# Side work by weighted steps in the chunk stage of an RWKV-7, retention and attention stack; the turn of YN and the state product at other levels

## The chip, the core and the metric

The kernel runs on one NeuronCore of a Trainium2 chip. The time is device microseconds of one launch, from the first instruction to the last with what lies around them; a profile's span is the first to the last instruction alone. Smaller is better.

## What is computed

The reference is two blocks of two layers each, at batch 1, 512 tokens and width 1024, all in float32. The first block (`hybrid_layer`) runs three branches on one projection of the normed input: a causal pool mixer, retention in chunks of 128 and an RWKV-7 time mix with 8 heads of 64. Three gates mix them, `w_out` projects the result, and an `adaLN` modulation (`w_ada`) surrounds it. The second block is a feed-forward, a conv and attention mixer and another feed-forward, each with a layer norm. The change touches only the RWKV-7 recurrence of the first block:

```python
def step(S, inp):
    r_t, w_t, k_t, v_t, a_t, b_t = inp
    sa = jnp.einsum('bhvk,bhk->bhv', S, a_t)
    S = (S * w_t[:, :, None, :] + sa[..., None] * b_t[:, :, None, :]
         + v_t[..., None] * k_t[:, :, None, :])
    return S, jnp.einsum('bhvk,bhk->bhv', S, r_t)
_, y = lax.scan(step, jnp.zeros((B, H, N, N), jnp.float32), xs)
y = head_norm(y, RWKV_NORM_EPS).reshape(B, T, BRANCH_W) * ln_w + ln_b
```

## The kernel before

**Engines and lanes.** Each engine has a class (`TensorE`, `VectorE`, `ScalarE`, `Pool`, `Sync`) that writes out its own instructions in program order. The classes walk through generators of the same shape (`chunks`, `chunk`, `retention`, `branch`, ...), and each `yield` is a place where `mix` may put in steps of a second generator. So one table of steps sets the order of all four engines, and semaphores, named by keys such as `("cw", at, lv)`, tie them together. An engine works strictly in its own order.

**Weights.** Every large matmul is done in three parts (`three`, L487 to L489): a float32 operand is split into a high and a low half. A unit of weights is 128 by 1024. ScalarE makes its high half (`whi`, L1747) and VectorE its low half (`wlo`, L997, the helper's line that nearly all of VectorE's two-operand work shares). There are four buffers for halves, so a unit is halved when the last matmul of the unit four before it is done. A step of side work is as a rule one `three` of 512 columns; eight of them use up a unit.

**The chunk stage.** It occurs once in each of the two layers of the first block. The main generator is `chunks`: four chunks of 128 tokens by two groups of four heads, eight bodies of `chunk` in a layer. Here the recurrence inside a chunk is a triangular inverse. One body does, on TensorE (its keys in brackets): the products of the chunk, which VectorE masks into `G` and from which it makes the first `U` (cg, L784); turns of B and K (cn); then six levels, n = 2 to 64. A level is a turn of U (ct, L493), which ScalarE copies to X; X by G (cy, L769), which ScalarE copies to Y; and Y by U (cw, L769), which VectorE copies into U (L1399 by a mask, for the last two levels L1405). Then come the product with the state (cW, L816, which needs `SP`, the state times its decay), the solve (cS), the state's update (cK) and the output (cY). VectorE then makes the mean and the variance of the output in `YN`, and GpSimd the inverse root.

**The tail.** The output of a body is finished inside the next one. VectorE scales `YN`, TensorE turns it (cT), ScalarE applies the layer norm's weights (two ACTIVATE into `KH`), and VectorE adds the result into `KH` (`tail_end`), which gives the bank of cT free.

**Banks.** All of these TensorE results go round banks 4 to 7 (`self.ps`). The fourth result after cT takes cT's bank again: with cT behind level 0 that is the turn of U of level 2.

**Side work.** `side` is the rest of the branch work: retention, gates, projections, and the `w_ada` products of two columns. `mix(self.chunks(l), side, 186, SIDE[l])` spreads 345 side steps in layer 0 and 321 in layer 1 evenly over the 186 yields of `chunks` (23 in each body and 2 behind them).

Of the kernel before, what the change touches and what calls it, by code (L numbers as in the profile page):

```python
# [11 lines left out]
ALU = mybir.AluOpType  # L12
# [164 lines left out]
def mix(main, side, main_steps, side_steps):  # L177

    done = n = 0
    for _ in main:  # L180
        n += 1
        while done < side_steps and done * main_steps < n * side_steps:
            next(side, None)
            done += 1
    for _ in range(done, side_steps):
        next(side, None)
# [162 lines left out]
SIDE = (345, 321)  # L349
LEVELS = tuple(enumerate((2, 4, 8, 16, 32, 64)))  # L350
# [103 lines left out]
class TensorE(Lane):  # L454
# [160 lines left out]
    def layer_a(self, l, nxt):  # L615
        k = self.k
        st = ("A", l)
        wa = tuple(x for d in range(8) for x in ((128 * d, 3584, 64), (128 * d, 4672, 64)))
        self.halves([("wa", l), ("wr", l, 0), ("pu", l, 0), ("pz", l, 0)], "w_in", (l,),
                    [wa, t_pieces(3072), t_pieces(0), t_pieces(512)], st)  # L620
        side = itertools.chain(self.pool(l), self.branch(l, 0, 1))
        mix(self.rwkv(l), side, 37, 144)
        drain(side)
        self.at(("ch", l))
        side = itertools.chain(self.retained(l), weave(itertools.chain(
            self.retention(l), self.last_gates(l), self.branch(l, 1, 2), self.out_gates(l)), self.adas_of(l), 8))
        mix(self.chunks(l), side, 186, SIDE[l])
        drain(side)
        self.at(("out", l))
        self.mark(("hlast", nxt))  # L630
        drain(weave(self.branch(l, 2, 8), self.rows(l + 1) if l + 1 < DEPTH else iter(()), 8))
        self.at(("wo", l))
        self.w_out(l, nxt)
# [138 lines left out]
    def chunk(self, l, c, g):  # L772
        k, e = self.k, self.e
        at, last = (l, c, g), (l, c - 1 + g, 1 - g)
        cs = slice(c * 128, (c + 1) * 128)
# [18 lines left out]
        for lv, n in LEVELS:  # L794
            bank = self.bank(self.ps, ("ct", at, lv))
            self.wait_ge(("cu", at, lv))
            self.turn(bank, [U[:, i * 128:(i + 1) * 128] for i in range(4)], ("ct", at, lv))
            yield
            bank = self.bank(self.ps, ("cy", at, lv))
            self.wait_ge(("cx", at, lv))  # L800
            self.four(bank, lambda i: G4[:, i * 512:i * 512 + 128], lambda i: X[:, i * 64:(i + 1) * 64], ("cy", at, lv))
            yield
            bank = self.bank(self.ps, ("cw", at, lv))
            self.wait_ge(("cyy", at, lv))
            self.four(bank, blk(Y), lambda i, n=n: PART(U[:, i * 128:(i + 1) * 128], 1, n), ("cw", at, lv))
            yield
            if lv == 0 and (c or g):
                self.tail(*last)
        S0 = k.SP
        vn = lambda h: k.VN[:, c * 512 + h * 64:c * 512 + (h + 1) * 64]  # L810
# [21 lines left out]
        if c < 3:  # L832
            bank = self.bank(self.ps, ("cK", at))
            self.wait_ge(("cnn", "BN", at), ("cnn", "KN", at), ("cSA", at))
            for i, (h, p, q) in enumerate(heads):
                o = bank[q:q + 64, (p - 2 * g) * 64:(p - 2 * g) * 64 + 64]
                e.matmul(o, k.BN[:, i * 64:(i + 1) * 64], SA(i), start=True, stop=False, skip_group_check=True)
                t = e.matmul(o, k.KN[:, i * 64:(i + 1) * 64], vn(h), start=False, stop=True, skip_group_check=True)
# [155 lines left out]
class VectorE(Lane):  # L994
# [114 lines left out]
    def layer_a(self, l, nxt):  # L1109
        k = self.k  # L1110
        st = ("A", l)
        used = self.halves(st)
        self.wait_ge(*([("xd", t) for t in range(4)] if l else []))
        self.e.memset(k.PP[:, 0:1], 0.0).then_inc(*self.up(("pp0", l)))
        self.give_back(used[:1])
        for i in used[1:]:
            self.spend(i)
        side = itertools.chain(self.pool(l), self.branch(l, 0, 1))
        mix(self.rwkv(l), side, 37, 144)
        drain(side)  # L1120
        self.at(("ch", l))
        side = itertools.chain(self.retained(l), weave(itertools.chain(
            self.retention(l), self.last_gates(l), self.branch(l, 1, 2), self.out_gates(l)), self.adas_of(l), 8))
        mix(self.chunks(l), side, 186, SIDE[l])
        drain(side)
        self.at(("out", l))
        if l + 1 < DEPTH:
            self.mod_columns(l + 1)
        self.rwkv_out(l)
        drain(weave(self.branch(l, 2, 8), self.rows(l + 1) if l + 1 < DEPTH else iter(()), 8))  # L1130
        self.at(("wo", l))
        self.w_out(l, nxt)
# [239 lines left out]
    def chunk(self, l, c, g):  # L1372
# [17 lines left out]
        for lv, n in LEVELS:  # L1390
            yield
            yield
            nb = 64 // n
            wb = k.bank(("cw", at, lv))
            self.wait_ge(("cw", at, lv), ("lmask",))
            if n < 32:
                m = (k.lmask[:, lv * 64:(lv + 1) * 64].rearrange("p (b n) -> p b n", n=n)
                     .unsqueeze(1).broadcast_to([128, 4, nb, n]))
                e.copy_predicated(FOUR_PART(U, 1, n), m, TIGHT(wb, n)).then_inc(  # L1399
                    *self.up(("cu", at, lv + 1), ("free", ("cw", at, lv))))  # L1400
            else:
                for b in range(nb):
                    s = 2 * n * b
                    self.wait_ge()
                    e.tensor_copy(V4(U)[s:s + n, :, s + n:s + 2 * n], TIGHT(wb, n)[s:s + n, :, b, :]).then_inc(  # L1405
                        *self.up(*([("cu", at, lv + 1), ("free", ("cw", at, lv))] if b == nb - 1 else [])))
            yield
            if c or g:
                if lv == 0:
                    self.tail(*last)  # L1410
                if lv == 1:
                    self.tail_end(*last)
        em = k.em[:, 32 * g:32 * g + 32].rearrange("p (t j c) -> p t j c", t=2, j=4)
        bc = lambda j: em[:, :, j, c].unsqueeze(2).broadcast_to([128, 2, 64])
        st = k.st[:, g * 128:(g + 1) * 128].rearrange("p (t v) -> p t v", t=2)
        spt = k.SP[:, :].rearrange("p (t j v) -> p t j v", t=2, j=2)
        if c == g == 0:
            self.wait_ge()
            e.memset(k.SP[:, :], 0.0).then_inc(*self.up())
        for j in range(2) if c else ():  # L1420
            q = slice(64 * j, 64 * j + 64)
            self.wait_ge()
            self.tt(spt[q, :, j, :], st[q, :, :], bc(0)[q, :, :], ALU.mult).then_inc(*self.up(*([("cs", at)] if j else [])))
        yield
        yield
        if c < 3:
# [9 lines left out]
            else:  # L1436
# [16 lines left out]
        self.tt(k.X[:, 256:512].rearrange("p (h n) -> p h n", h=4), vn,  # L1453
                k.bon[:, c * 8 + 4 * g:c * 8 + 4 * g + 4].unsqueeze(2).broadcast_to([128, 4, 64]), ALU.mult).then_inc(*self.up())
        yield

    def tail(self, l, c, g):
        k = self.k
# [280 lines left out]
class ScalarE(Lane):  # L1739
# [68 lines left out]
    def layer_a(self, l, nxt):  # L1808
        k = self.k
        st = ("A", l)  # L1810
        used = self.halves(st)
        self.give_back(used[:1])
        for i in used[1:]:
            self.spend(i)
        self.wait_ge(("x", st, 3), *([("xd", t) for t in range(4)] if l else []))
        side = itertools.chain(self.pool(l), self.branch(l, 0, 1))
        mix(self.rwkv(l), side, 37, 144)
        drain(side)
        self.at(("ch", l))
        side = itertools.chain(self.retained(l), weave(itertools.chain(  # L1820
            self.retention(l), self.last_gates(l), self.branch(l, 1, 2), self.out_gates(l)), self.adas_of(l), 8))
        mix(self.chunks(l), side, 186, SIDE[l])
        drain(side)
        self.at(("out", l))
        self.rwkv_out(l)
        drain(weave(self.branch(l, 2, 8), self.rows(l + 1) if l + 1 < DEPTH else iter(()), 8))
        self.at(("wo", l))
        self.w_out(l, nxt)
# [152 lines left out]
    def chunk(self, l, c, g):  # L1981
        k = self.k
# [9 lines left out]
        for lv, n in LEVELS:  # L1992
            key = ("ct", at, lv)
            self.wait_ge(key, *before)
            self.e.copy(TIGHT(X, n), FOUR_PART(k.bank(key), 0, n)).then_inc(*self.up(("cx", at, lv), ("free", key)))  # L1995
            yield
            key = ("cy", at, lv)
            self.wait_ge(key, ("cz", l))
            self.e.copy(FOUR_PART(Y, 0, n), TIGHT(k.bank(key), n)).then_inc(*self.up(("cyy", at, lv), ("free", key)))  # L1999
            yield  # L2000
            yield
            if lv == 0 and (c or g):
                self.tail(*last)
        key = ("cW", at)
        self.wait_ge(key)
# [200 lines left out]
class Pool(Lane):  # L2206
# [40 lines left out]
    def layer_a(self, l, nxt):  # L2247
# [8 lines left out]
        if l:  # L2256
# [7 lines left out]
        self.e.memset(k.Y[:, :], 0.0).then_inc(*self.up(("cz", l)))  # L2264
        side = itertools.chain(self.retained(l), weave(itertools.chain(
            self.retention(l), self.last_gates(l), self.branch(l, 1, 2), self.out_gates(l)), self.adas_of(l), 8))
        mix(self.chunks(l), side, 186, SIDE[l])
        drain(side)
        self.at(("out", l))
        self.wait_ge(*ALL(("out", l)))  # L2270
# [47 lines left out]

    def chunk(self, l, c, g):
        hs = self.k.hs  # L2320
        yield from self.steps(22)
        self.rstd(hs[:, 8:12], hs[:, 4:8], 1.0 / 64, 64e-5, [("cvar", (l, c, g))], ("crs", (l, c, g)))
        yield

# [151 lines left out]
```

## Time and profile before

| | before |
|---|---|
| median of 3 runs | 3810.29 us (3807.25 to 3812.89) |
| the profiled execution's own time | 3813.6 us |
| its span | 3811.8 us |
| mean granted TensorE clock | 0.951 |
| chunk stage of layer 0 | about 341 to 870 us |
| chunk stage of layer 1 | about 1206 to 1706 us |

The two stages can be found in the trace by the tile U, which is used nowhere else. A wait in the trace is idle time of an engine right before an instruction, with the engine, tile and line whose end let it go.

### The profile page before, as it was taken

The page shows a single profiled execution, that of the slowest core. Times are in us where ns is not written, and L with a number is a line of the kernel's source. Part 1 is how long each engine was busy: PE and PEld are TensorE (multiplying, and loading weights), DVE is VectorE, ACT ScalarE, POOL GpSimd, SP SyncE. Part 2 cuts the span into 40 slices and gives each one's busy share as a digit, 9 for nine tenths or more (in the row PEclk, how much of TensorE's full clock was granted, in tenths as well). Part 3 has the DMA queues.
Part 4 walks back from the last instruction along what each step waited for, and adds up shares of the span by engine and source line. Part 5 has one row for each costly group of instructions (what it writes and reads, how often), then busy time and mean ns, then how long its engine had stood idle before and what let it go on. Part 6 is the DMA issues. An engine that isn't in the chain of part 4 may idle for free. (4 is left out here: it accounts for less than half of the span.)

```text
span 3811.8 us, 43469 instructions
## 1 busy us (share of the span) xinstructions
PE 3462.5 (91%) x17192; PEld 2808.8 (74%) x17192; DVE 1790.3 (47%) x2485; ACT 1147.3 (30%) x1671; POOL 174.5 (5%) x232
## 2 busy tenths in 40 slices
PE   4889888988888888989999977999999997889999
PEld 2767777776667767778888855888888886668887
DVE  5564554346655554345333474533243327644333
ACT  3433223222343222223332224223122312333321
POOL 1000000000000000000000110000000002000000
PEclk7989999999999999999999987999999999889999
DMA  4122111223222111122323211232323321113232
GB/s 167 61 74 76 56 56 63 76 72 103 89 72 72 56 56 39 46 79 81 102 97 107 96 45 34 83 100 95 107 86 100 101 98 64 50 45 100 99 106 78
DMA packets 83803, 303.72 MB, mean 80 GB/s; under 512 B 9856, under 2 KB 10128, under 8 KB 83600
## 3 DMA queue, kind: packets, MB, share of 16 engines
q1 hardware_dynamic: 78048, 282.59, 22.3%
q0 software_dynamic: 5552, 18.35, 1.5%
q8 instruction: 136, 2.23, 0.2%
q14 instruction: 67, 0.55, 0.0%
HBM read 296.19 MB, written 4.72 MB: 79 GB/s over the span
## 5 line engine op out<-in xcount | busy, mean ns | idle before, releaser
L487 PE MATMUL bank<-hh,whi 128*128 128x512 f32 (+1 forms) x2880 | 1133.3, 393 | 99.2 <-DVE wlo L997 40.1
L489 PE MATMUL bank<-hh,wlo 128*128 128x512 f32 (+1 forms) x2880 | 1090.3, 379 | 0.0
L488 PE MATMUL bank<-hl,whi 128*128 128x512 f32 (+1 forms) x2880 | 1090.0, 378 | 0.0
L997 DVE TENSOR_TENSOR wlo<-raw,whi 128x1024 fp32r<-128x1024 f32 x530 | 650.3, 1227 | 932.9 <-ACT whi L1747 864.9
L1747 ACT CAST whi<-raw 128x1024 fp32r<-128x1024 f32 x530 | 556.2, 1049 | 839.6 <-PE bank L489 722.3
L487 PEld LDWEIGHTS bank<-hh,whi 128*128 128x128 f32 x2880 | 559.4, 194 | 223.8 <-issue 72.5
L489 PEld LDWEIGHTS bank<-hh,wlo 128*128 128x128 f32 x2880 | 558.5, 194 | 98.8
L488 PEld LDWEIGHTS bank<-hl,whi 128*128 128x128 f32 x2880 | 560.0, 194 | 85.2 <-issue 3.6
L487 PE MATMUL bank<-whi,fh 128*128 128x512 f32 x704 | 278.3, 395 | 0.0
L489 PE MATMUL bank<-whi,fl 128*128 128x512 f32 x704 | 277.8, 395 | 0.0
L488 PE MATMUL bank<-wlo,fh 128*128 128x512 f32 x704 | 277.7, 395 | 0.0
L997 DVE TENSOR_TENSOR tmp<-tmp,bank 128x512 f32<-128x512 f32 x104 | 71.6, 688 | 244.0 <-PE bank L489 241.6
L2076 ACT CAST fh<-tmp 128x512 fp32r<-128x512 f32 x88 | 54.6, 621 | 375.4 <-DVE tmp L997 375.4
L487 PEld LDWEIGHTS bank<-whi,fh 128*128 128x128 f32 x704 | 132.6, 188 | 30.9
L489 PEld LDWEIGHTS bank<-whi,fl 128*128 128x128 f32 x704 | 132.6, 188 | 30.8
L488 PEld LDWEIGHTS bank<-wlo,fh 128*128 128x128 f32 x704 | 132.7, 188 | 30.7
L769 PEld LDWEIGHTS bank<-X,G 128*128 128x128 f32 x768 | 107.1, 206 | 22.6 <-ACT X L1995 14.4
L493 PE MATMUL bank<-ident,U 128*128 128x128 f32 x384 | 62.9, 289 | 56.2 <-DVE U L997 26.3
L769 PEld LDWEIGHTS bank<-U,Y 128*128 128x128 f32 x768 | 98.7, 192 | 20.0 <-ACT Y L1999 13.2
L1399 DVE COPY_PREDICATED U<-lmask,bank 128x256 f32<-128x256 uint32 x64 | 32.5, 508 | 170.7 <-PE bank L769 169.8
L769 PE MATMUL bank<-X,G 128*128 128x64 f32 x768 | 106.6, 286 | 5.6 <-ACT X L1995 5.4
L493 PEld LDWEIGHTS bank<-ident,U 128*128 128x128 f32 x384 | 46.2, 146 | 79.3 <-DVE U L997 33.2
(302 smaller groups left out, 3850.5 us busy)
## 6 DMA issues: line engine op xcount, KB each, us to landing
raw<-in_W SPq DMA_DIRECT2D x530, 512.0 KB, 3.3
bc<-in_ln_g POOLq DMA_DIRECT2D x6, 512.0 KB, 4.3
bc<-in_ln_b POOLq DMA_DIRECT2D x6, 512.0 KB, 5.5
xn<-in_x SPq DMA_DIRECT2D x4, 512.0 KB, 8.6
xn<-in_x POOLq DMA_DIRECT2D x4, 512.0 KB, 5.5
xd<-xn POOLq DMA_DIRECT2D x4, 512.0 KB, 3.4
xn<-xd POOLq DMA_DIRECT2D x4, 512.0 KB, 5.3
out<-xn SPq DMA_DIRECT2D x4, 512.0 KB, 2.6
```

Source lines behind the costliest of these rows:

```text
L487: e.matmul(out, ah, bh, start=first, stop=False, skip_group_check=True)
L488: e.matmul(out, ah, bl, start=False, stop=False, skip_group_check=True)
L489: return e.matmul(out, al, bh, start=False, stop=last, skip_group_check=True)
L493: t = self.e.transpose(bank[:, j * 128:(j + 1) * 128], x, self.k.ident[:, :])
L769: t = self.e.matmul(bank[:, i * 64:(i + 1) * 64], lhs(i), rhs(i), start=True, stop=True, skip_group_check=True)
L997: return self.e.tensor_tensor(o, a, b, op)
L1399: e.copy_predicated(FOUR_PART(U, 1, n), m, TIGHT(wb, n)).then_inc(*self.up(("cu", at, lv + 1), ("free", ("cw", at, lv))))
L1747: self.e.copy(self.k.halves(i)[0], self.k.raw_unit(n)).then_inc(*self.up(("hi", i)))
L2076: self.e.copy(HALF(k.fh, m), tm).then_inc(*self.up(("fh", st, m)))
```

## The change

`mix` now adds up what the main generator yields: a plain `yield` counts 1, a `yield 2` counts 2. The yield behind cw in each of the six levels becomes `yield 2`, on all four engines. The total goes from 186 to 234 (29 in each body and 2), and the number of side steps stays the same, so a plain yield gets 345/234 = 1.47 steps instead of 1.85 in layer 0, and the yield behind cw gets 2.95. The tail of the body before (the scaling and turn of `YN`) moves from behind level 0 to behind level 1. Its end (`tail_end`) moves from behind level 1 to behind level 2. The product of the state with its decay (`SP`), which stood behind level 5, becomes a method `state` and stands behind level 3.

```diff
 def mix(main, side, main_steps, side_steps):
     done = n = 0
-    for _ in main:
-        n += 1
+    for w in main:
+        n += w or 1
         while done < side_steps and done * main_steps < n * side_steps:
             next(side, None)
             done += 1
...
-        mix(self.chunks(l), side, 186, SIDE[l])
+        mix(self.chunks(l), side, 234, SIDE[l])
...
             self.four(bank, blk(Y), lambda i, n=n: PART(U[:, i * 128:(i + 1) * 128], 1, n), ("cw", at, lv))
-            yield
-            if lv == 0 and (c or g):
+            yield 2
+            if lv == 1 and (c or g):
                 self.tail(*last)
...
-            yield
+            yield 2
             if c or g:
-                if lv == 0:
+                if lv == 1:
                     self.tail(*last)
-                if lv == 1:
+                if lv == 2:
                     self.tail_end(*last)
+            if c and lv == 3:
+                self.state(l, c, g)
...
-        for j in range(2) if c else ():
-            q = slice(64 * j, 64 * j + 64)
-            self.wait_ge()
-            self.tt(spt[q, :, j, :], st[q, :, :], bc(0)[q, :, :], ALU.mult).then_inc(*self.up(*([("cs", at)] if j else [])))
...
+    def state(self, l, c, g):
+
+        k = self.k
+        st = k.st[:, g * 128:(g + 1) * 128].rearrange("p (t v) -> p t v", t=2)
+        spt = k.SP[:, :].rearrange("p (t j v) -> p t j v", t=2, j=2)
+        before = k.em[:, 32 * g:32 * g + 32].rearrange("p (t j c) -> p t j c", t=2, j=4)[:, :, 0, c].unsqueeze(2).broadcast_to(
+            [128, 2, 64])
+        for j in range(2):
+            q = slice(64 * j, 64 * j + 64)
+            self.wait_ge()
+            self.tt(spt[q, :, j, :], st[q, :, :], before[q, :, :], ALU.mult).then_inc(*self.up(*([("cs", (l, c, g))] if j else [])))
...
             self.e.copy(FOUR_PART(Y, 0, n), TIGHT(k.bank(key), n)).then_inc(*self.up(("cyy", at, lv), ("free", key)))
             yield
-            yield
-            if lv == 0 and (c or g):
+            yield 2
+            if lv == 1 and (c or g):
                 self.tail(*last)
...
-        yield from self.steps(22)
+        yield from self.steps(2)
+        for _ in LEVELS:
+            yield from self.steps(2)
+            yield 2
+        yield from self.steps(2)
```

What this does to the order is shown at three places. The first is VectorE in the third body of layer 0 (c = 1, g = 0), from the copy of level 1 on. `qr`, `sw` and the BN instructions are retention's, `wlo` is a low half. Before:

```order
L1399 COPY_PREDICATED U<-lmask,bank 128x64x4
L997 TENSOR_TENSOR KH<-KH,bank 128x2x128
L1399 COPY_PREDICATED U<-lmask,bank 128x32x8
L997 TENSOR_TENSOR qr<-bank,cosr 128x512
L997 TENSOR_TENSOR sw<-bank,sinr 64x512 x2
L997 TENSOR_TENSOR qr<-qr,sw 128x512
L1264 BN_STATS stat<-bank 128x6 x4
L1267 BN_AGGR stat<-stat 128x2 x4
L997 TENSOR_TENSOR wlo<-raw,whi 128x1024 x2
L1399 COPY_PREDICATED U<-lmask,bank 128x16x16
```

After, the same stretch of VectorE:

```order
L1399 COPY_PREDICATED U<-lmask,bank 128x64x4
L997 TENSOR_TENSOR YN<-YN,hs 128x256
L1399 COPY_PREDICATED U<-lmask,bank 128x32x8
L997 TENSOR_TENSOR qr<-bank,cosr 128x512
L997 TENSOR_TENSOR sw<-bank,sinr 64x512 x2
L997 TENSOR_TENSOR qr<-qr,sw 128x512
L1264 BN_STATS stat<-bank 128x6 x4
L1267 BN_AGGR stat<-stat 128x2 x4
L997 TENSOR_TENSOR wlo<-raw,whi 128x1024 x2
L997 TENSOR_TENSOR KH<-KH,bank 128x2x128
L1399 COPY_PREDICATED U<-lmask,bank 128x16x16
L1000 TENSOR_SCALAR sw<-bank,stat 128x128 x4
```

The addition into `KH`, which frees the bank of cT, stood right behind the copy of level 1 and now stands behind retention's block and two low halves. The second place is TensorE at the same point, from cw of level 2 (the first row) to the turn of U of level 3 (L493). L726 is retention's product. Before:

```order
L769 MATMUL bank<-U,Y 128x64 x4
L487 MATMUL bank<-hh,whi 128x512
L488 MATMUL bank<-hl,whi 128x512
L489 MATMUL bank<-hh,wlo 128x512
L487 MATMUL bank<-hh,whi 128x512
L488 MATMUL bank<-hl,whi 128x512
L489 MATMUL bank<-hh,wlo 128x512
L493 MATMUL bank<-ident,U 128x128 x4
L726 MATMUL bank<-vret,pt 128x128 x10
```

After:

```order
L769 MATMUL bank<-U,Y 128x64 x4
L487 MATMUL bank<-hh,whi 128x512
L488 MATMUL bank<-hl,whi 128x512
L489 MATMUL bank<-hh,wlo 128x512
L487 MATMUL bank<-hh,whi 128x512
L488 MATMUL bank<-hl,whi 128x512
L489 MATMUL bank<-hh,wlo 128x512
L726 MATMUL bank<-vret,pt 128x128 x10
L487 MATMUL bank<-hh,whi 128x512
L488 MATMUL bank<-hl,whi 128x512
L489 MATMUL bank<-hh,wlo 128x512
L493 MATMUL bank<-ident,U 128x128 x4
```

Two steps before the turn of U have become three steps and retention's product. The third place is TensorE at the start of the last body of layer 1, from the last product of the chunk (L784) to the turns of B and K. Before:

```order
L784 MATMUL bank<-AR,KH 128x256
L487 MATMUL bank<-hh,whi 128x512
L488 MATMUL bank<-hl,whi 128x512
L489 MATMUL bank<-hh,wlo 128x512
L487 MATMUL bank<-hh,whi 128x512
L488 MATMUL bank<-hl,whi 128x512
L489 MATMUL bank<-hh,wlo 128x512
L493 MATMUL bank<-ident,BH 128x128 x2
L493 MATMUL bank<-ident,KH 128x128 x2
```

After:

```order
L784 MATMUL bank<-AR,KH 128x256
L487 MATMUL bank<-hh,whi 128x512
L488 MATMUL bank<-hl,whi 128x512
L489 MATMUL bank<-hh,wlo 128x512
L493 MATMUL bank<-ident,BH 128x128 x2
L493 MATMUL bank<-ident,KH 128x128 x2
```

One step less lies between them. Counted over the whole order of TensorE in both stages, in steps of three matmuls (a mean over the 16 bodies, or the 96 levels):

| from, to | before | after |
|---|---|---|
| turn of U, X by G (ct to cy) | 1.58 | 1.25 |
| X by G, Y by U (cy to cw) | 1.50 | 1.22 |
| cw to the next turn of U, no tail between | 1.59 | 2.45 |
| cw to the turn of YN | 1.36 | 2.64 |
| end of a body to cg | 1.50 | 0.93 |
| cg to the turns of B and K | 1.62 | 1.44 |
| those to the first turn of U | 1.69 | 1.19 |

## Rows read from the trace of the kernel before

**Rows 1.** Page: busy us, share and instructions of each engine

```profile
PE 3462.5 (91%) x17192; PEld 2808.8 (74%) x17192; DVE 1790.3 (47%) x2485; ACT 1147.3 (30%) x1671; POOL 174.5 (5%) x232
```

**Rows 2.** Windows of the two chunk stages (times, span, engines' busy us, clock)

```profile
341.00:870.00 529.00, 473.95 (x2772) 384.10 (x2772) 235.18 (x394) 147.69 (x259) 25.94 (x29) 0.95 0.20 66
1206.00:1706.00 500.00, 446.43 (x2676) 365.17 (x2676) 217.66 (x380) 129.45 (x237) 22.36 (x29) 0.97 0.16 54
```

**Rows 3.** Waits of TensorE, 341 to 1706: total us, times, longest

```profile
PE bank L493 <- DVE U L997: 26.3, 14, 5.6
PE bank L493 <- DVE YN L997: 20.8, 9, 5.3
PE bank L493 <- DVE KH L997: 11.7, 9, 2.6
PE bank L493 <- DVE U L1405: 10.7, 7, 3.5
...
PE bank L816 <- DVE SP L997: 7.7, 5, 3.3
PE bank L493 <- DVE U L1399: 7.4, 7, 3.1
...
PE bank L769 <- ACT X L1995: 5.4, 8, 1.2
...
PE bank L493 <- DVE G L997: 5.1, 9, 2.5
PE bank L769 <- ACT Y L1999: 4.8, 8, 1.4
```

**Rows 4.** Timeline: turns of YN behind the last body of each layer

```profile
843.53 0.44 PE L493 MATMUL bank<-ident,YN 128*128 128x128 f32 x2 [2.86 <-DVE YN L997]
...
1678.03 0.56 PE L493 MATMUL bank<-ident,YN 128*128 128x128 f32 x2 [2.84 <-DVE YN L997]
```

**Rows 5.** Timeline: one halving ahead of the copy of U (layer 1)

```profile
1583.87 0.37 ACT L1999 COPY Y<-bank 128x256 f32<-128x256 f32 x1 [1.31 <-PE bank L769]
...
1584.33 1.05 ACT L1747 CAST whi<-raw 128x1024 fp32r<-128x1024 f32 x1
...
1585.51 1.22 DVE L997 TENSOR_TENSOR wlo<-raw,whi 128x1024 fp32r<-128x1024 f32 x1 [1.05 <-ACT whi L1747]
...
1586.77 0.43 DVE L1399 COPY_PREDICATED U<-lmask,bank 128x256 f32<-128x256 uint32 x1
...
1587.23 0.42 DVE L997 TENSOR_TENSOR KH<-KH,bank 128x256 f32<-128x256 f32 x1
...
1587.70 0.55 PE L493 MATMUL bank<-ident,U 128*128 128x128 f32 x3 [0.90 <-DVE KH L997]
```

**Rows 6.** Timeline: retention's block on VectorE behind level 2, third body of layer 0

```profile
494.59 0.60 PE L493 MATMUL bank<-ident,U 128*128 128x128 f32 x4
494.86 0.69 DVE L997 TENSOR_TENSOR qr<-bank,cosr 128x512 f32<-128x512 f32 x1 [1.01 <-PE bank L489]
495.02 2.40 PE L726 MATMUL bank<-vret,pt 128*128 128x128 f32 x20
...
497.17 0.48 PE L487 MATMUL bank<-hh,whi 128*128 128x512 f32 x1
...
500.01 2.54 DVE L997 TENSOR_TENSOR wlo<-raw,whi 128x1024 fp32r<-128x1024 f32 x2
...
502.58 0.45 DVE L1399 COPY_PREDICATED U<-lmask,bank 128x256 f32<-128x256 uint32 x1
```

**Rows 7.** Timeline of TensorE behind a wait of 4.50 us

```profile
535.85 1.09 PE L493 MATMUL bank<-ident,U 128*128 128x128 f32 x4 [4.50 <-DVE U L997]
536.58 0.78 PE L487 MATMUL bank<-hh,whi 128*128 128x512 f32 x1
...
541.73 0.40 PE L489 MATMUL bank<-hh,wlo 128*128 128x512 f32 x1
541.96 0.39 PE L487 MATMUL bank<-hh,whi 128*128 128x512 f32 x1
```

More of the change, by code:

```diff
@@ L1123, in layer_a @@
             self.retention(l), self.last_gates(l), self.branch(l, 1, 2), self.out_gates(l)), self.adas_of(l), 8))
-        mix(self.chunks(l), side, 186, SIDE[l])
+        mix(self.chunks(l), side, 234, SIDE[l])
         drain(side)
@@ L1415, in chunk @@
         st = k.st[:, g * 128:(g + 1) * 128].rearrange("p (t v) -> p t v", t=2)
-        spt = k.SP[:, :].rearrange("p (t j v) -> p t j v", t=2, j=2)
         if c == g == 0:
@@ L1821, in layer_a @@
             self.retention(l), self.last_gates(l), self.branch(l, 1, 2), self.out_gates(l)), self.adas_of(l), 8))
-        mix(self.chunks(l), side, 186, SIDE[l])
+        mix(self.chunks(l), side, 234, SIDE[l])
         drain(side)
@@ L2266, in layer_a @@
             self.retention(l), self.last_gates(l), self.branch(l, 1, 2), self.out_gates(l)), self.adas_of(l), 8))
-        mix(self.chunks(l), side, 186, SIDE[l])
+        mix(self.chunks(l), side, 234, SIDE[l])
         drain(side)
```

## The prediction

> **What bounds the kernel now.** I read the page first: TensorE is busy for 91% of the span, VectorE for 47%, ScalarE for 30% [rows 1]. No work is added or taken away by this change, so the time can only move through TensorE's idle time and its clock. Second, the windows of the two chunk stages, the only places where the order changes: of 529 and 500 us TensorE is busy 473.95 and 446.43, so 108.6 us are idle, and VectorE is busy for 44% of both, with a granted clock of 0.95 and 0.97 [rows 2]. No engine is the bound there but TensorE. Third, the waits of TensorE over that stretch, sorted by who ended them. The reader is to see that nearly all end with VectorE's handing over something of the chunk: the first U of a body 26.3 us, the masked G 5.1, YN 20.8, the copies of U inside the levels 7.4 and 10.7, the addition into KH 11.7, SP 7.7; ScalarE's X and Y cost 5.4 and 4.8 [rows 3]. All of these name instructions that only the chunk stages have. The DMA does not appear.
>
> VectorE is not short of time; it is late because in its own order something long stands ahead of the piece that TensorE wants. So what counts is what stands ahead of each such piece, and how much TensorE has to do meanwhile (its cover). A `three` step is worth 3 x 0.23 = 0.70 us (two matmuls start at 541.73 and 541.96) [rows 7].
>
> **The change part by part.**
>
> *SP.* The state product goes two levels forward. Its five waits, 7.7 us [rows 3], end: behind level 3 it has two levels of TensorE work ahead of its first reader. It costs VectorE nothing new. **-7.7 us.**
>
> *Turn of YN, one level later.* Of the 20.8 us [rows 3], 2.86 and 2.84 are those behind the last bodies [rows 4], which don't move. That leaves 15.1. At level 1 the order shows five bodies with side work between the copy of U and YN (two with two low halves, one with a low half and a `pt`, two with retention's four `sw`), and the 1.28 steps of cover that are added behind cw help all bodies. I put what remains at 10, from the chain priced below (the double halvings 2.5 and 3.9, the one with `pt` 1.7, lateness elsewhere 2): **-5 us**, between -15 and 0.
>
> *Turns of U.* From cw to the next turn the cover grows from 1.59 to 2.45 steps, 0.6 us. The waits on the two copies are 7.4 + 10.7 = 18.1 us in 14 pieces [rows 3]. 14 x 0.6 would be 8.4. Besides, side work now falls behind the copy more often, where a whole level covers it. Against that, a block ahead of the copy has less cover in the other two gaps. **-9 us**, between -4 and -15.
>
> *Bank of cT.* This is where I see the loss. The turn of U that comes three results later waits until `tail_end` has added into KH. Before, `tail_end` stood behind level 1, and in the order of VectorE nothing stood between the copy of U and it in all but two of the 14 bodies that have it inside. After, it stands behind level 2, with three steps' worth of side work ahead of it, and the order shows side work there in 11 of 14 (about 31 us of VectorE's time by the rows' durations, where it was under 2). This work can't be hidden behind a level: `tail_end` must come before the next turn of U, and the cover is the gap alone.
> The price of one halving there: ScalarE's high half 1.05, VectorE's low half 1.22, KH 0.42, with the hand-overs some 2.9 us [rows 5], from the end of the unit; cover is the rest of the gap, 0.7 to 2.1 us. So 0.8 to 2.2 us each, 0.6 more where ScalarE has a gate's sigmoid first. Those rows show the same with the halving ahead of cw: a wait of 0.90 at twice the cover. Nine bodies are of about this kind or have a small block; worked through one by one, about 17 us.
> Three bodies have retention's block. The first of these is the place shown in the order: the block starts when its unit ends at 494.59, and its low halves end at 500.01 + 2.54 = 502.55, 8.0 us later. KH makes it 8.4. Before, it stood ahead of the copy of level 3 and had a whole level as cover, and the copy at 502.58 held nobody up [rows 6]. After, TensorE has ahead of the turn of U retention's product, 497.17 - 495.02 = 2.15 us [rows 6], and one step: 2.85. A wait of about 5.5 us. The same block in layer 1 with one low half less makes 4.3; the second half of the block (the third body's successor, `kr`, `ol`, `wlo` ahead of KH) about 4.8. Together 14.6.
> 32 in place of 11.7: **+20 us**. Below, +5 (if VectorE runs the block in the gaps of its waits for TensorE), above +24.
>
> *Start of a body.* From the output to the first turn of U TensorE has 1.50 + 1.62 + 1.69 = 4.81 steps before and 0.93 + 1.44 + 1.19 = 3.56 after, 1.25 less, 0.87 us. VectorE's part (YN, G, U) is fixed and already the longer one: G and the first U hold TensorE for 31.4 us, U in 14 of 16 bodies [rows 3]. 14 x 0.87 = 12.2; some 3 us of side work leave VectorE's stretch with it. **+9 us**, between +4 and +12.
>
> *X, Y and the end of a body.* Gaps of one step rather than two become the rule on the two copies of ScalarE. They cost 10.2 us over 192 gaps [rows 3], few of them long. A high half that falls between two copies (1.05 us [rows 5]) was covered by 1.4 us and is not by 0.7. **+4 us**, between 0 and +10.
>
> *Clock.* Behind the wait of 4.50 us the granted clock is at the lower level, 1.2 GHz: four transposes take 1.09 us [rows 7] instead of 0.60 [rows 6], and the upper level, 2.4 GHz, is back about 5 us later (0.39 per matmul). Such a stretch gives away half its length, some 2 us. Waits above 2.4 us are about as many as before by my list (SP's and YN's go, KH's come): **0**, between -6 and +6.
> The Trainium skill, page "TensorE: Matmul & The Clock Gate", section "HAM oscillation — how this bites in real kernels", says the same of the price: the extra wall time is the throttled time times (1 - 1.2/2.4). The trace agrees at that place. By this rule the change would pay wherever it breaks up the longest waits, even at equal idle time; that is a rival below.
>
> Sum: -7.7 - 5 - 9 + 20 + 9 + 4 = +11.3. Neighbouring waits overlap (while TensorE stands at KH, ScalarE and VectorE catch up for the next X, Y and U), for which I take off 3: **+8 us**. The profiled execution took 3813.6, which is 3.3 above the median; against it that is 3821.6, against the median of 3810.3 it is 3818.
>
> The Trainium skill, page "Perfetto Trace Analysis", section "Optimization Strategy", advises to find the gaps of the busiest engine, see which semaphore ends them, and let that dependency start sooner. By it the turn of U is the right target (18.1 us). The rows say it is a fifth of the idle time, and that more hangs on the start of a body and on KH.
>
> **The rivals.** (A measurement of this kernel tells 0.2%, 7.6 us, from no change.)
>
> *1. Forecast: the waits for KH and at the start of a body outweigh the gains.* +3 to +20 us. Chance 0.53, two thirds of it above the 7.6.
>
> *2. The other side, faster: the gap behind cw really is the place where lateness is made.* For it: SP and YN are gains that I can name by instruction, together up to 7.7 + 15.1 = 22.8, and the turns of U give up to 15. Against it: the block at 494.86. It decides at KH. If its waits stay at about 12 us, the sum is +11.3 - 20 = -9, so 3802; with the U and YN terms at their best ends -25, 3785. The point at which the sign turns is KH at 20 us. Chance 0.22.
>
> *3. A draw: the idle time only changes its name.* VectorE's long blocks are the same and meet TensorE's next hand-over wherever that is; the nine small cases come out at 1 us rather than 1.9. Then KH stands at about 24, the sum is near +1, 3811. Chance 0.17.
>
> *4. The clock.* The clock falls short by 0.05 x 529 + 0.03 x 500 = 41 us in the two stages, a part of it while TensorE stands still [rows 2], and the long waits at SP and YN (up to 3.3 and 5.3 [rows 3]) are of the kind that rows 7 show. If four or five stretches of 2 us go and none comes, 8 to 10 us are gained beside rival 3's balance: 3802. If the KH waits of 4 to 5.5 us and longer ones at the first U (5.6 now [rows 3]) each draw one, 6 more are lost on top of the forecast: 3824. The gain has a chance of 0.03, the loss one of 0.05.
>
> **The numbers.** Most likely 3818. The forecast's own range is 3813 to 3830. The range for 8 in 10 reaches into rivals 2 and 4: 3799 to 3832. Faster by over 0.2% (below 3802.7): rival 2 and the gain of 4, 0.25. Slower (above 3817.9): two thirds of the forecast and the loss of 4, 0.40. Within: the rest, 0.35.
>
> **What would show it.** In the waits of TensorE: SP gone; YN about 16 with the two tails; L1399 and L1405 together about 9; KH from 11.7 to 25 or more, with single waits of 4 to 5 us in the third and fourth body of layer 0 and the fourth of layer 1, right behind retention's product; first U and G at about 40; X and Y at 13 to 16. The clock of the two windows stays at 0.95 to 0.97. I am wrong if KH stays below 20 or the start of a body doesn't move; in the first case `tail_end` runs earlier than its place in the order makes me think.

## The result, and the profile after

The changed kernel takes 3844.65 us, median of 4 runs (3841.62 to 3848.38), beside 3810.78 us for the kernel before in the same comparison. The ratio is 1.0091, with a 95% interval of 1.0076 to 1.0107: slower by 34 us. The direction was forecast; the size was not, and lies outside the range. The profiled execution took 3841.62, its span 3839.8.

The page of the changed kernel, busy time by engine, answers to [rows 1]. TensorE is busy 16 us longer with the same instructions:

```profile
PE 3478.6 (91%) x17192; PEld 2817.9 (73%) x17192; DVE 1790.2 (47%) x2485; ACT 1148.0 (30%) x1671; POOL 175.5 (5%) x232
```

The windows of the two chunk stages of the changed kernel (times, length, then busy us of TensorE, its weight loads, VectorE, ScalarE and GpSimd, the granted clock, DMA share, GB/s) answer to [rows 2]:

```profile
338.50:879.00 540.50, 481.16 (x2772) 386.72 (x2773) 237.27 (x397) 149.03 (x261) 29.09 (x33) 0.94 0.21 65
1214.00:1739.00 525.00, 461.70 (x2676) 375.22 (x2676) 217.43 (x379) 129.26 (x237) 23.87 (x32) 0.94 0.16 51
sum 1065.50, PE 942.86 PEld 761.95 DVE 454.71 ACT 278.29 POOL 52.96; mean PE 471.43 PEld 380.97 DVE 227.35 ACT 139.15 POOL 26.48
```

Cut at the same events (341 to 872 and 1208 to 1708), the stages of the kernel before are 1031.0 us with TensorE busy for 920.4. So the stages hold the whole loss, 34.5 us (the two profiled executions are 28.0 us apart; outside the stages the changed one is 6.5 us shorter), and it has two parts: idle time goes from 110.6 to 122.6 (+12.0), and busy time from 920.4 to 942.9 (+22.5) for equal work. The clock of the two windows fell from 0.95 and 0.97 to 0.94 and 0.94.

The waits of TensorE from 341 to 1730 (in total, times, longest, us) answer to [rows 3]:

```profile
PE bank L493 <- DVE KH L997: 33.5, 12, 5.4
PE bank L493 <- DVE U L997: 28.1, 14, 7.0
PE bank L493 <- DVE YN L997: 22.1, 13, 4.4
...
PE bank L769 <- ACT X L2004: 7.8, 13, 1.6
...
PE bank L493 <- DVE U L1405: 5.2, 4, 2.0
PE bank L769 <- ACT Y L2008: 5.1, 7, 2.0
...
PE bank L493 <- DVE G L997: 4.6, 10, 2.1
...
PE bank L493 <- DVE U L1399: 2.2, 2, 1.2
```

SP is gone from the list, and KH has become its head. The timeline at the place where the prediction put the largest wait for KH, both engines, is the next view (start, duration, engine, line, operation, tiles, count, and in brackets the idle time before). VectorE works off two low halves, then adds into KH, and only then may the turn of U take the bank:

```profile
485.96 2.54 DVE L997 TENSOR_TENSOR wlo<-raw,whi 128x1024 fp32r<-128x1024 f32 x2
...
488.54 0.42 DVE L997 TENSOR_TENSOR KH<-KH,bank 128x256 f32<-128x256 f32 x1
489.01 1.12 PE L493 MATMUL bank<-ident,U 128*128 128x128 f32 x4 [5.38 <-DVE KH L997]
...
491.21 1.80 PE L769 MATMUL bank<-X,G 128*128 128x64 f32 x8
...
494.19 0.63 PE L487 MATMUL bank<-hh,whi 128*128 128x512 f32 x1
...
494.62 0.44 PE L488 MATMUL bank<-hl,whi 128*128 128x512 f32 x1
494.90 0.39 PE L489 MATMUL bank<-hh,wlo 128*128 128x512 f32 x1
```

Behind the wait four transposes take 1.12 us and a 512-column matmul 0.63, where they take 0.60 and 0.39 at the upper level; that lasts 5.6 us. Such a stretch can also follow a shorter wait and last longer, as TensorE's timeline of the changed kernel shows at 634:

```profile
634.33 0.84 PE L493 MATMUL bank<-ident,U 128*128 128x128 f32 x4 [2.37 <-DVE KH L997]
...
636.38 1.86 PE L595 MATMUL bank<-ones,gate 2*128 2x1 f32 x8
638.17 1.97 PE L769 MATMUL bank<-X,G 128*128 128x64 f32 x8
...
641.33 1.80 PE L769 MATMUL bank<-U,Y 128*128 128x64 f32 x8
...
644.31 0.63 PE L487 MATMUL bank<-hh,whi 128*128 128x512 f32 x1
...
645.05 0.40 PE L489 MATMUL bank<-hh,wlo 128*128 128x512 f32 x1
```

This one is 10.4 us long. The granted clock of the trace has the same place at 0.50, and at 1.00 behind it (the same columns as in the windows above):

```profile
634.66:644.88 10.22, 10.22 (x38) 8.78 (x37) 1.01 (x3) 0.91 (x3) 0.00 (x0) 0.50 0.16 53
644.90:654.90 10.00, 10.00 (x60) 7.80 (x59) 1.79 (x3) 2.76 (x5) 0.00 (x0) 1.00 0.16 52
```

In the text from here on, **low clock** is the time in the two stages over which the 512-column matmuls of the `three` steps take more than 0.6 us, each stretch counted from the first such matmul to the next faster one: 55.7 us before, 89.2 after. Half of the difference, 16.7 us, is its price. This measure misses the edges of the stretches. **Granted low** is TensorE's busy time inside the stretches over which the trace's granted clock is 0.50: 72.6 us before, 115.8 after. Half of that difference is 21.6 us, so the clock is nearly all of the 22.5.

Which stretches grew can be listed by the durations, if every product is counted and not the 512-column ones alone (which gives 66.0 us before and 99.8 after). Two stretches followed a wait for KH before, 6.9 us; seven do after, 43.5 us. All others together went from 59.1 to 56.3. So the low clock that was added lies behind the waits for KH. That the waits are its cause is shown by e4_end_first, below.

### The profile page after: what moved, and what is told of

The parts are those of the page before. It is cut to its first block and busy times, and to the rows that moved or that the text cites. A ratio compares the mean times of both kernels' runs of the same rounds, so it can differ in the third digit from the quotient of the medians.

```text
span 3839.8 us, 43480 instructions
## 1 busy us (share of the span) xinstructions
PE 3478.6 (91%) x17192; PEld 2817.9 (73%) x17192; DVE 1790.2 (47%) x2485; ACT 1148.0 (30%) x1671; POOL 175.5 (5%) x232
## 3 DMA queue, kind: packets, MB, share of 16 engines
q1 hardware_dynamic: 78048, 282.59, 22.5%
## 5 line engine op out<-in xcount | busy, mean ns | idle before, releaser
L1399 DVE COPY_PREDICATED U<-lmask,bank 128x256 f32<-128x256 uint32 x64 | 32.6, 509 | 230.4 <-PE bank L769 229.8
L493 PE MATMUL bank<-ident,U 128*128 128x128 f32 x384 | 64.5, 294 | 69.0 <-DVE KH L997 33.5
L493 PEld LDWEIGHTS bank<-ident,U 128*128 128x128 f32 x384 | 48.2, 150 | 90.3 <-DVE KH L997 38.7
```

What stands on the lines that cost most here:

```text
L493: t = self.e.transpose(bank[:, j * 128:(j + 1) * 128], x, self.k.ident[:, :])
```

## The experiments

The kernel before ran beside each group of them, with medians of 3810.8 to 3814.7, so small differences are read from the ratios. Idle time is the stages' length less TensorE's busy time, from the two windows of each run; the expectations' idle time is the sum of the waits with a known releaser, some 4 us less. Times are us.

| kernel | median | ratio to before, 95% | stages | busy | idle | low clock | granted low |
|---|---|---|---|---|---|---|---|
| before | 3810.8 | | 1031.0 | 920.4 | 110.6 | 55.7 | 72.6 |
| changed | 3844.7 | 1.0091 (1.0076 to 1.0107) | 1065.5 | 942.9 | 122.6 | 89.2 | 115.8 |
| e1_state | 3801.5 | 0.9967 (0.9957 to 0.9977) | 1020.6 | 918.3 | 102.3 | 49.9 | 72.2 |
| e2_tail | 3836.2 | 1.0058 (1.0039 to 1.0077) | 1051.2 | 926.1 | 125.1 | 61.7 | 85.5 |
| e3_weights | 3847.0 | 1.0087 (1.0066 to 1.0107) | 1068.8 | 943.5 | 125.3 | 102.0 | 118.7 |
| e4_end_first | 3798.7 | 0.9958 (0.9945 to 0.9971) | 1020.3 | 926.6 | 93.7 | 63.1 | 84.0 |
| e5_tail_back | 3807.8 | 0.9983 (0.9974 to 0.9993) | 1023.5 | 921.3 | 102.3 | 58.6 | 73.7 |
| e6_both_first | 3793.5 | 0.9943 (0.9928 to 0.9958) | 1016.2 | 930.5 | 85.7 | 75.7 | 92.7 |
| e7_even_both_first | 3781.5 | 0.9916 (0.9901 to 0.9931) | 1003.7 | 909.2 | 94.5 | 40.3 | 54.5 |
| e8_w3 | 3788.5 | 0.9938 (0.9923 to 0.9953) | 1010.2 | 924.2 | 86.0 | 58.0 | 73.5 |
| e9_w15 | 3780.0 | 0.9915 (0.9901 to 0.9930) | 996.9 | 909.3 | 87.7 | 44.1 | 53.8 |
| e10_even_tail0 | 3785.2 | 0.9929 (0.9914 to 0.9943) | 1005.5 | 909.3 | 96.2 | 44.8 | 52.7 |
| e11_w2_ct | 3818.7 | 1.0019 (1.0009 to 1.0028) | 1040.1 | 932.0 | 108.1 | 87.4 | 98.6 |
| e12_filled | 3774.4 | 0.9901 (0.9885 to 0.9918) | 996.7 | 923.1 | 73.7 | 38.1 | 54.5 |

### One part at a time

**e1_state**: the kernel before, with the product of the state and its decay behind level 3.

```diff
+            if c and lv == 3:
+                self.state(l, c, g)
...
```

> The kernel before with one part of the change: the state product (SP) behind level 3 of the inversion in place of behind level 5. Theory A (the loss of the change lies in the addition into KH, which now stands behind a gap full of side work, and in the low-clock stretches that its waits draw): this part is a plain gain. The five SP waits (7.7 us) go, and with the two of 2.9 and 3.3 us perhaps two low-clock stretches of 4 us, worth 2 us each: 3799 to 3804. Theory B (the loss comes from the uneven spread of the side steps itself: shorter plain gaps at the start of a body and around X and Y): the same here. Rival to both: the wait only moves on to the next hand-over of VectorE, 3808 to 3812.

The waits for SP are gone and no other moved by more than 0.5 us. The stages are 10.4 us shorter.

**e2_tail**: the kernel before, with the tail and its end one level later, in even steps.

```diff
             yield
-            if lv == 0 and (c or g):
+            if lv == 1 and (c or g):
                 self.tail(*last)
...
             yield
-            if c or g:
-                if lv == 0:
-                    self.tail(*last)
-                if lv == 1:
-                    self.tail_end(*last)
+            if (c or g) and lv == 1:
+                self.tail(*last)
+            if (c or g) and lv == 2:
+                self.tail_end(*last)
...
```

> The kernel before with one part of the change: the tail one level later (YN turned behind level 1, its end behind level 2), with even steps. In the order about 18 us of VectorE's side work stand ahead of the addition into KH in 7 of the 14 bodies that have it inside (under 2 us in 2 bodies before, about 31 us in 11 bodies in the changed kernel). Theory A: the KH waits rise from 11.7 to 20 to 26 us, two of them at 5 us, YN falls by 8 to 12 us; 3806 to 3820. Theory B: moving the tail is harmless and YN's gain shows: 3800 to 3804.

Slower by 22 us, more than either theory had; this part alone makes the kernel slower. KH goes from 11.7 to 25.1, as theory A had it, but YN only from 20.8 to 17.7, and L1399 goes up from 7.4 to 11.2.

**e3_weights**: the kernel before, with `yield 2` behind cw and the total of 234, and nothing else of the change.

> The kernel before with one part of the change: weight 2 behind each level's last product, with tail and state product where they were. Theory A: KH waits stay at 10 to 17 us, YN at 15 to 22, the copies of U fall from 18 to about 9, the start of a body costs a few us more; 3806 to 3822. Theory B: this part carries most of the loss: 3832 to 3846.

Theory A fell as it was worded. The turns of U do gain (L1399 and L1405 together 7.1, from 18.1), but what the change puts first in the list of waits is SP:

```profile
PE bank L493 <- DVE U L997: 30.1, 15, 7.0
PE bank L816 <- DVE SP L997: 25.1, 8, 7.1
PE bank L493 <- DVE YN L997: 18.6, 7, 4.6
```

The double portion of side work behind level 5 stands ahead of the state product, which its readers want at once. In the full change the state had moved away from there.

**e5_tail_back**: the changed kernel with the tail where it was: weights and the early state.

```diff
             yield 2
-            if lv == 1 and (c or g):
+            if lv == 0 and (c or g):
                 self.tail(*last)
...
             yield 2
-            if c or g:
-                if lv == 1:
-                    self.tail(*last)
-                if lv == 2:
-                    self.tail_end(*last)
+            if (c or g) and lv == 0:
+                self.tail(*last)
+            if (c or g) and lv == 1:
+                self.tail_end(*last)
...
```

> The changed kernel with the tail where it was (YN turned behind level 0, its end behind level 1); weights and the early state product stay. Set against the changed kernel it prices the move of the tail under weights, set against the run with weights alone it prices the state product under weights. In that run KH cost 16.1 us, YN 18.6 and SP 25.1. If the waits add up without moving: SP's 25 go, KH and YN stay near 16 and 19, idle time of the two stages about 97 us against 118 in the changed kernel, time 3808 to 3822. If the waits only move on to the next hand-over, or if the spread of steps is itself the loss: 3830 and above.

This closes the decomposition. From before to e1_state the early state gives -0.33% (-12.6 us). From there to e5_tail_back the weights cost 0.16% (+6), and the two intervals overlap. From there to the changed kernel the tail's later level costs 1.08% (+41). The last step is 42.0 us in the stages: 20.3 of idle time (KH 16.1 to 33.5, YN 18.6 to 22.1) and 21.6 of busy time, with the low clock going from 58.6 to 89.2 and granted low from 73.7 to 115.8. And e3_weights less e5_tail_back, which differ in the state's place alone, is 45.3 us in the stages, again half idle (23.0) and half busy time (22.2).

### The order inside the gap

**e4_end_first**: the changed kernel with `tail_end` right behind the copy of level 2, ahead of the gap's side work.

```diff
+            if (c or g) and lv == 2:
+                self.tail_end(*last)
             yield 2
-            if c or g:
-                if lv == 1:
-                    self.tail(*last)
-                if lv == 2:
-                    self.tail_end(*last)
+            if (c or g) and lv == 1:
+                self.tail(*last)
```

> The changed kernel with one edit: VectorE makes the addition into KH (tail_end) right behind the copy of level 2, ahead of the weighted gap's side work, not behind it. All engines' other work stays in its order. Theory A: the KH waits (33.5 us in the changed kernel) fall to under 5 us, and the low-clock time in the two stages goes back towards that of before (mean granted clock of the two stages from 0.94 back to 0.95 to 0.97); 3800 to 3815. Theory B: the KH waits go but come back under other names, and the time stays at 3832 or above.

3798.66 us: 46 us less than the changed kernel by the medians, 51 by the ratios (0.9958 beside 1.0091) and 45.2 in the stages, by the place of one instruction per body. At the block of the prediction the timeline of e4_end_first reads:

```profile
479.67 0.43 DVE L1399 COPY_PREDICATED U<-lmask,bank 128x256 f32<-128x256 uint32 x1 [5.94 <-PE bank L769]
...
480.13 0.42 DVE L997 TENSOR_TENSOR KH<-KH,bank 128x256 f32<-128x256 f32 x1
...
480.84 2.39 PE L726 MATMUL bank<-vret,pt 128*128 128x128 f32 x20
481.11 0.69 DVE L997 TENSOR_TENSOR qr<-bank,cosr 128x512 f32<-128x512 f32 x1 [0.55 <-PE bank L489]
...
483.76 0.60 PE L493 MATMUL bank<-ident,U 128*128 128x128 f32 x4
```

The addition stands ahead of retention's block, and the turn of U starts without a wait at the upper level. KH falls from 33.5 to 1.4 us. The stages lose 28.9 us of idle time and 16.3 of busy time, and granted low falls from 115.8 to 84.0, of which half is 15.9: a microsecond of waiting for KH cost 1.4.

**e6_both_first**: as e4_end_first, and the scaling of YN too stands ahead of the gap's side work, behind the copy of level 1.

> The changed kernel with both of VectorE's parts of the tail ahead of the weighted gap's side work: the scaling of YN right behind the copy of level 1, the addition into KH right behind that of level 2. Against the run with only the latter, YN's waits inside the bodies (16 us) fall to about 3: 12 to 16 us less and perhaps some low-clock time, 3780 to 3790. If the wait only moves on to the next hand-over of VectorE: 3795 to 3800.

YN falls from 22.1 to 12.0, not to 3, and idle time to 85.7. But busy time rises by 3.9, and of the 10 us won in waits 5 arrive by the medians and 4.1 in the stages; the two ratios' intervals overlap. The time lies between the two ranges expected.

**e7_even_both_first**: the same with even steps (plain yields, total 186): the changed kernel's two moves without its weights, and both of VectorE's parts ahead of the side work.

> As the run before this one, but with even steps (weight 1): state product behind level 3, tail one level later, both of VectorE's parts of the tail ahead of the gap's side work. It prices the weights with the tail and the state product out of their way. If the weights are a gain once nothing stands behind the gap (the copies of U in time), this is 4 to 12 us slower than the weighted one. If they cost (starts of bodies, X and Y, and small products packed closer, with more time at the lower clock for the same idle time), it is 3 to 12 us faster than the weighted one, 3772 to 3785, with the low-clock stretches of the two stages at 50 us or less in all, where the weighted kernels so far have 63 to 102.

12 us faster than e6_both_first although it has 8.8 us more idle time. The copies of U are waited for 22.2 us again (11.5 and 10.7; 18.1 before the change); against that stand 21.3 us less busy time. The windows of e6_both_first, then those of e7_even_both_first:

```profile
338.10:854.80 516.70, 474.32 (x2773) 381.38 (x2773) 237.33 (x397) 149.27 (x261) 29.18 (x33) 0.95 0.21 68
1189.80:1689.30 499.50, 456.14 (x2676) 372.04 (x2677) 217.41 (x379) 129.46 (x237) 24.11 (x33) 0.95 0.17 53
```

```profile
339.90:856.20 516.30, 465.82 (x2772) 378.37 (x2773) 237.29 (x397) 149.26 (x261) 28.07 (x33) 0.96 0.21 68
1192.00:1679.40 487.40, 443.35 (x2677) 364.86 (x2677) 217.42 (x379) 129.48 (x237) 24.14 (x33) 0.98 0.17 55
```

**e10_even_tail0**: as e7_even_both_first with the tail at levels 0 and 1.

> Even steps, both parts first, the state behind level 3, and the tail where it stood before the change (levels 0 and 1). Theory A, the tail's level is worth little once both parts stand ahead of the gap's side work: KH 4 to 12 us, YN 15 to 19 us, within 8 us of the kernel with even steps and the tail one level later, 3780 to 3792 us. Theory B, the later level itself pays: 3795 us or more.

3785.2, ratio 0.9929 beside 0.9916 with the later level: the intervals overlap. KH is 9.0 and YN 15.3. Once both parts stand ahead of the gap's side work, the level is worth nothing that can be told here. This run differs from e1_state in that order alone, and there it is worth 0.38% (14 us): idle time goes from 102.3 to 96.2 and busy time from 918.3 to 909.3.

### Weights and the clock

**e8_w3** and **e9_w15**: as e6_both_first with weight 3 (total 282) and 1.5 (total 210).

> Weight 3 instead of 2 behind the copy of W, both YN's scaling and the end of the chain ahead of the gap's side work. Theory A, packing the side work behind W costs clock: idle in the two chunk stages 75 to 83 us, low clock 90 us or more (75.7 with weight 2), 3800 to 3815 us. Theory B, the clock follows the waits of 2 us and more alone: low clock 65 to 76 us, 3785 to 3795 us.

> As with weight 2 and both parts first, weight 1.5. Theory A (packing costs clock): between the two kernels that stand beside it, low clock 45 to 65 us, idle 83 to 88 us, 3783 to 3792 us. Theory B (waits alone): low clock with the number of waits of 2 us and more, and with fewer waits than even steps have, at or under 3780 us.

With weights 1, 1.5, 2 and 3 the idle time is 94.5, 87.7, 85.7 and 86.0, as it should be, and the low clock is 40.3, 44.1, 75.7 and 58.0 (granted low 54.5, 53.8, 92.7 and 73.5). Theory A falls: weight 1.5 has hardly more low clock than even steps, at B's 3780.0 us, and weight 3 takes 3788.5, below A's range. But B, by which the low clock goes with the waits of 2 us and more, does not hold either: those are 13, 10, 10 and 11 inside the stages with the four weights (the wait at either end of a stage left out), and with weight 2, where only 6 reach 2.4 us, the low clock is nearly twice that of even steps, where all 13 do. So uneven steps can cost some 35 us at the lower level, and no rule of these two says at which weight. How weights 2 and 3 differ is not shown: their ratios overlap, and over all four runs of each the mean granted clock is 0.952, 0.951, 0.949 and 0.950 with the four weights, while the one run with weight 2 that was profiled had 0.947.

**e11_w2_ct**: as e6_both_first, with the weight 2 behind ct in place of cw.

> Both parts first, weight 2 behind the copy of T instead of W: the side work is as uneven as in the changed kernel, at another place. Theory A, unevenness anywhere costs clock: low clock 65 to 80 us, idle 85 to 95 us (copies of U and turns of U at 11 us and more again), 3795 to 3810 us. Theory B, only the gap behind W matters: low clock 40 to 50 us, 3780 to 3790 us.

3818.7 us, slower than either theory had it. The low clock is 87.4, so the gap behind cw is not special: the same unevenness elsewhere costs as much or more. The idle time is 108.1, also more than expected, with L1405 at 15.0 in 6 and KH back at 9.9 in 7:

```profile
PE bank L493 <- DVE U L1405: 15.0, 6, 4.8
PE bank L493 <- DVE YN L997: 13.2, 10, 2.9
PE bank L493 <- DVE KH L997: 9.9, 7, 4.3
```

**e12_filled**: as e9_w15, with TensorE given something to do while it would wait for the first U of a body.

```diff
             bank = self.bank(self.ps, ("ct", at, lv))
+            for i in range(8) if lv == LEVELS[0][0] else ():
+                e.transpose(bank[:, (i % 4) * 128:(i % 4 + 1) * 128], self.k.ident[:, :], self.k.ident[:, :])
             self.wait_ge(("cu", at, lv))
```

> As with weight 1.5 and both parts first (3780.0 us; idle 83.4, low clock 44.1 us), with eight transposes of the identity, 1.1 us at the upper level, ahead of the first turn of U of each of the 16 bodies, into the bank that the turn overwrites: added work, no result changes. It stands in the wait on the first U (29.0 us in 15). Theory A, standing still draws the low clock: idle falls by 13 to 16 us, the stretches behind the first U (15.3 us in three) shrink, low clock 30 to 40 us, and the time falls by 3 to 7 us, to 3773 to 3777. Theory B, the small products draw it and standing still does not: idle falls likewise, low clock stays at 44 or rises, and the time is 3779 to 3786.

(The three stretches named there come to 13.8 us in all, not 15.3, when they are counted as in e12_filled.) The wait for the first U falls from 29.0 in 15 to:

```profile
PE bank L493 <- DVE U L999: 15.1, 7, 6.0
```

Idle time falls by 14.0, and the low clock from 44.1 to 38.1; the stretches behind the first U go from 13.8 to 8.2 us. Standing still thus may have a part in those. But the granted clock does not bear out a gain in all: it stands at 0.50 for 61.4 us of the two stages in e9_w15 and for 61.8 here, for at other places it fell where it had not before, and granted low is 53.8 and 54.5. So neither theory is shown. The length of the stages does not move, 996.7 beside 996.9: busy time rises by 13.8, as much as the idle time falls. The median is 5.6 lower, but the intervals of the two ratios overlap, and the stages do not show it.

## Why the prediction was right in direction and wrong in size

**The step that failed** is the clock: "Waits above 2.4 us are about as many as before by my list (SP's and YN's go, KH's come): 0, between -6 and +6." It measured +22.5 us of busy time, 21.6 of it by the granted clock (16.7 by the matmuls' durations). The count in it was no worse than said: waits of 2.4 us and more inside the two stages went from 16 to 13, those of 2 us and more from 17 to 20. The inference fell. A stretch is not 5 us at each such wait: before, 17 stretches were 3.9 us long in the mean; after, 21 of 4.8, from under 1 to 10.4 us, five of them behind no wait of 2 us (two of these five behind one of 1.97 and 1.99). The price I gave for one (half its length) held; it was their number and length that I took as fixed. Rival 4's loss, "if the KH waits of 4 to 5.5 us ... each draw one", is what happened, with seven stretches at KH rather than three. I gave it 0.05 and 6 us.

The Trainium skill, page "TensorE: Matmul & The Clock Gate", section "HAM oscillation — how this bites in real kernels", prices throttled time at half. The traces of this case agree: busy time less half of granted low is 882 to 888 us in the thirteen kernels without filler (887 to 898 less half the low clock), while the busy time itself runs from 909 to 943.

**The sum of the idle terms** was +11.3 and measured +12.0. By its terms:

- *Bank of cT*, 11.7 to 32: measured 33.5. (The turn of U that waits is the fourth result after cT, not the third; nothing else hung on it.) The three blocks, forecast at 5.5, 4.8 and 4.3, are 5.38 (489.01), 4.67 (561.70) and 4.06 (1437.63). e4_end_first confirms the cause, side work ahead of the addition.
- *SP*, -7.7: right (e1_state). What I did not see is that the weights would have made it 25.1 had the state stayed (e3_weights).
- *Turns of U*, 18.1 to 9: measured 7.4, and it is the weights that do it (7.1 in e3_weights, 7.2 in e5_tail_back).
- *Turn of YN*, to about 16: measured 22.1, no gain. The later level brought its own side work: in even steps it gives 3.1 (e2_tail), under weights it costs 3.5 (e5_tail_back to the changed kernel). e6_both_first shows the rest of the cause: ahead of the side work it is 12.0.
- *Start of a body*, 31.4 to 40: measured 32.7. Of the +9, 1.3 came, or 2.9 with a wait for the state at L784 (1.6) that the kernel before does not have. The weights add some 4 us there (25.7 in e7_even_both_first and 29.6 in e6_both_first for U), not 9; why so little, no run settles.
- *X, Y and the end*, 10.2 to 13 to 16: measured 12.9 at the products (7.8 and 5.1), and 16.0 with two waits at the end of a body (2.1 and 1.0), which were 1.3 before and which the 10.2 leaves out.
- *Overlap*, -3: no sign of it in the sum.

The terms for YN and for the start of a body missed by 6 and 8 in opposite directions, so a part of the sum's fit is luck. The reading that the turns of U are a fifth of the idle time was loose: 18.1 of 108.6 is a sixth.

**Rival 2** (faster, if KH stays low) was sound in its condition: with KH at 1.4 the kernel is faster, by 0.42% (e4_end_first). **Rival 3** would have had KH near 24.

**What is open.** Why one stretch at the lower level lasts 2.3 us and another 10.4; why the weights 1, 1.5, 2 and 3 give 40, 44, 76 and 58 us; and why no more was lost at the start of a body. Each kernel has one profile behind these sums, and it can lie some microseconds off the median (e5_tail_back's is the fastest of its ten runs, 6 us below). That e6_both_first is slower than e7_even_both_first with less idle time is no accident of one profile: the four runs of each don't overlap (3791.0 to 3793.6 beside 3778.7 to 3788.2), though the intervals of the two ratios just do.

## What to carry to other kernels

An instruction that hands over a bank or an operand goes ahead of the side work of its gap, on the engine that hands over. That one line was worth 46 us here, where a weighted gap stood ahead of it, and both such lines 14 us with even steps and the tail at its old level. Both lines, even steps, the early state and the later level make a kernel 0.84% faster than before (e7_even_both_first), of which the early state alone gives 0.33%; the weights and the later level on which the change spent itself are worth little or cost. When a wait on the bounding engine is priced, the slow stretch behind it belongs to the price: here 1.4 us for each microsecond at KH. And parts are to be tried alone and together: the weights' cost at SP (waits of 25.1 us in place of 7.7) is seen only without the early state, that of the tail doubles with the weights (+22 alone, +41 with them).

## What the runs showed of the hardware

The granted clock is not a function of the waits of 2 us and more alone. With fewer waits and less idle time than e7_even_both_first, e6_both_first has 35 us more at the lower level; six of its 16 stretches have no wait of 2 us in the 8 us ahead, and they are 5.0 us long in the mean, where e7_even_both_first has three of 13, of 2.9. Five of those six have a wait of 1.5 to 2.0 us ahead. The changed kernel has a stretch of 2.7 us at 795.4 behind a turn and two narrow products of the gates, with no wait longer than 0.3 us; e3_weights has one of 4.1 us at 795.0, the same place. Idle time filled with small transposes (e12_filled) took away less than half of the stretches' length behind it (13.8 to 8.2 us), and the time at the lower level in the two stages stayed as it was (61.4 and 61.8 us).
